# The order of fills, row maxima and weight splits in a hybrid DeltaNet and attention block

## The reference

```python
h = rmsnorm(x, norm_w[l])
proj = jnp.einsum('bsd,de->bse', h, w_in[l])
y_a = gated_deltanet(gdn_qkv, gdn_z, gdn_b, gdn_a, ...)
y_b = forgetting_attention(fox_q, fox_k, fox_v, fox_z, fox_f, ...)
g_a, g_b = jnp.split(jax.nn.sigmoid(gate_logit + gate_b[l]), 2, axis=-1)
merged = g_a * (y_a @ w_up_gdn[l]) + g_b * (y_b @ w_up_fox[l])
x = x + merged @ w_out[l]
return rmsnorm(x, final_norm_w)
```

## Time and profile before

| | |
|---|---|
| median of 3 runs | 1018.75 us (1017.97 to 1020.62) |
| the profiled execution, its own time | 1018.75 us |
| its span, first to last instruction | 1016.8 us |
| mean granted TensorE clock | 0.993 |
| TensorE busy | 960.7 us, 94% |
| VectorE, ScalarE busy | 604.8 us (59%), 464.6 us (46%) |
| edited loop, by TensorE | some 532 to 790 us |

### The profile page before, as it was taken

One profiled execution on the slowest core, in us unless ns is written; L12 is line 12 of the kernel. 1 busy time (PEld: TensorE's weight loads), 2 busy tenths in 40 slices (PEclk: granted clock), 3 DMA queues, 4 the chain that ended last, 5 costly groups with the idle time before them and its releaser, 6 DMA issues.

```text
span 1016.8 us, 15520 instructions
## 1 busy us (share of the span) xinstructions
PE 960.7 (94%) x6224; PEld 730.3 (72%) x6224; DVE 604.8 (59%) x949; ACT 464.6 (46%) x847; POOL 20.7 (2%) x28
## 2 busy tenths in 40 slices
PE   3899999999999999999789989999899999999997
PEld 2777787778888877777566656665565788888886
DVE  6367658799999623343368476675774342328162
ACT  6355655533555435422346546546455543334041
POOL 1000001020000000000000000000000000000000
PEclk9999999999999999999899999999999999999999
DMA  6111351148223662210453332333210523233062
GB/s 212 42 46 51 88 178 44 59 149 210 84 83 104 207 198 60 68 54 33 146 167 101 98 114 74 115 104 104 81 65 22 208 77 100 68 119 104 2 205 83
DMA packets 115039, 104.85 MB, mean 103 GB/s; under 512 B 33488, under 2 KB 95056, under 8 KB 114584
## 3 DMA queue, kind: packets, MB, share of 16 engines
q1 hardware_dynamic: 103304, 80.26, 27.0%
q10 hardware_dynamic: 10512, 19.40, 5.2%
q0 software_dynamic: 1152, 4.19, 1.3%
HBM read 76.84 MB, written 27.00 MB: 102 GB/s over the span
## 4 chain that ended last, share of the span: by engine, by line
PE 43%; ACT 3%; DVE 2%; issue 2%; DMA 1%; DVEq 0%; SPq 0%; ACTq 0%
PE pj L2042 6%; PE pj L2044 5%; PE pj L2043 5%; PE pc L2170 3%; PE pa L2143 2%; PE pa L2112 1%; PE pj L2053 1%; PE pj L2054 1%; PE pj L2055 1%; PE pb L2185 1%; DMA mst<-rows_scratch 1%; PE pb L2196 1%; PE pc L2307 1%; PE pb L2307 1%; PE pa L2307 1%
## 5 line engine op out<-in xcount | busy, mean ns | idle before, releaser
L143 PE MATMUL pj<-h_hi,w_hi 128*128 128x512 f32 x496 | 199.4, 402 | 4.2 <-ACT xc L492 2.3
L145 PE MATMUL pj<-h_hi,w_lo 128*128 128x512 f32 x496 | 193.6, 390 | 0.0
L144 PE MATMUL pj<-h_lo,w_hi 128*128 128x512 f32 x496 | 193.4, 390 | 0.0
L143 PEld LDWEIGHTS pj<-h_hi,w_hi 128*128 128x128 f32 x496 | 93.0, 188 | 27.8 <-issue 5.3
L2042 PE MATMUL pj<-h_hi,w_hi 128*128 128x512 f32 x256 | 107.2, 419 | 3.4 <-PEq L292 3.4
L145 PEld LDWEIGHTS pj<-h_hi,w_lo 128*128 128x128 f32 x496 | 93.1, 188 | 19.9
L144 PEld LDWEIGHTS pj<-h_lo,w_hi 128*128 128x128 f32 x496 | 93.2, 188 | 17.6
L2044 PE MATMUL pj<-h_hi,w_lo 128*128 128x512 f32 x256 | 101.7, 397 | 0.0
L2043 PE MATMUL pj<-h_lo,w_hi 128*128 128x512 f32 x256 | 101.5, 396 | 0.0
L2042 PEld LDWEIGHTS pj<-h_hi,w_hi 128*128 128x128 f32 x256 | 49.2, 192 | 25.9 <-issue 16.2
L599 ACT ACTIVATE xc<-pj 128x512 f32<-128x512 f32 x40 | 23.8, 596 | 94.5 <-PE pj L145 94.5
(11 more groups left out here) (317 smaller groups left out, 1836.3 us busy)
## 6 DMA issues: line engine op xcount, KB each, us to landing
w_raw<-in_w_in SPq DMA_DIRECT2D x48, 512.0 KB, 4.5
fox_scratch<-xc ACTq DMA_DIRECT2D x40, 256.0 KB, 2.1
qkv<-in_x SPq DMA_DIRECT2D x8, 512.0 KB, 6.8
fqk<-fox_scratch SPq DMA_DIRECT2D x8, 512.0 KB, 4.4
fa<-rows_scratch POOLq DMA_DIRECT2D x8, 512.0 KB, 5.5
rv<-fr_scratch SPq DMA_DIRECT2D x16, 256.0 KB, 4.1
m_scratch<-mst ACTq DMA_DIRECT2D x16, 256.0 KB, 2.8
ma<-m_scratch SPq DMA_DIRECT2D x8, 512.0 KB, 4.3
```

The costliest lines, as they stand in the source:

```text
L143: nc.tensor.matmul(o, w_hi[:, slot, k], h_hi[:, k, cols], start=(k == 0), stop=False)
L144: nc.tensor.matmul(o, w_hi[:, slot, k], h_lo[:, k, cols], start=False, stop=False)
L145: last = nc.tensor.matmul(o, w_lo[:, slot, k], h_hi[:, k, cols], start=False, stop=(k == KT - 1))
```

## The change

The count of operations on each engine stays as it was, and so does `FILLS`. TensorE: the eight fills around `turn_max(p, 0)` are 3, 4, 1 instead of 4, 4; in steps v = 0 to 3 the fills stand between slot v's scores and the short piece, and the values (or `turn_values`) behind the short piece; at v = 3 two fills stand there and two behind; `values(p, 3)` comes behind the next two slots' scores; `weight_sums(p, 0)` and `head_sums(p + 1)` change places, with the waits for the shared bank that go with it. ScalarE: the work on z is a step later, `squares`, `row_norms` two steps later, `sum_square(2 p)` two earlier. VectorE: the work on z stands behind the row maxima, `out_y(p - 1, 1)` ahead of `spread_max(p, 1)`, the output norm of the first half at v = 6 instead of 8, `normalise` at v = 10 and 11 instead of 8 and 10, `add_weights(p, 5)` a step earlier; the low parts of weights are made one step earlier. SP: loads of weights one step earlier and ahead of the norms in the queue, `load_v` ahead of `norm_rows`, both at v = 8 instead of 5, `norm_rows_k` at v = 10 instead of 8.

```diff
@@ SP
+                    for t in tiles_through(g - 2):
+                        load_raw(t + 3)
+                    for t in ups_through(g - 2):
+                        load_up(t + 3)
                     if v == 4 and p:
                         store_y(p - 1, 1)
-                    if v == 5 and p + 1 < PAIRS:
+                    if v == 8 and p + 1 < PAIRS:
+                        load_v(p + 1)
                         norm_rows(p + 1)
-                        load_v(p + 1)
-                    if v == 8 and p + 1 < PAIRS:
+                    if v == 10 and p + 1 < PAIRS:
                         norm_rows_k(p + 1)
-                    for t in tiles_through(g - 3):
-                        load_raw(t + 3)
-                    for t in ups_through(g - 3):
-                        load_up(t + 3)
@@ ScalarE
-                        if v == 1:
+                        if v == 2:
                             act.wait_ge(fz_loaded, 16 * p + 16)
...
-                        if v == 2:
+                        if v == 3:
                             act.wait_ge(z_step, 2 * p + 1)
...
-                        if v == 3 and p + 1 < PAIRS:
+                        if v == 5 and p + 1 < PAIRS:
                             squares(p + 1, 0, fq, q_loaded)
                             squares(p + 1, 1, fk, k_loaded)
-                        if v == 5 and p + 1 < PAIRS:
+                        if v == 5:
+                            sum_square(2 * p)
+                        if v == 7 and p + 1 < PAIRS:
                             row_norms(p + 1)
-                        if v == 7:
-                            sum_square(2 * p)
@@ VectorE
-                        if v >= 1 and slot(v - 1)[1] and v != 6:
-                            if v == 7:
-                                add_weights(p, 5)
+                        if v >= 1 and slot(v - 1)[1]:
                             add_weights(p, v - 1)
                         if 0 <= v < 4:
                             row_max(p, 4 + 2 * v)
-                            if v == 2:
-                                dve.wait_ge(z_act, 3 * p + 1)
-                                nc.vector.tensor_scalar(fv, fv, LN_MAX, 1.0, ALU.min, ALU.add).then_inc(z_step, 1)
-                            if v == 3:
-                                dve.wait_ge(z_act, 3 * p + 3)
-                                nc.vector.scalar_tensor_tensor(fz, fz, fox_nw["o"], fv, ALU.mult, ALU.mult).then_inc(z_step, 1)
                             row_max(p, 5 + 2 * v)
...
                     if g < STEPS:
+                        if v == 2:
+                            dve.wait_ge(z_act, 3 * p + 1)
+                            nc.vector.tensor_scalar(fv, fv, LN_MAX, 1.0, ALU.min, ALU.add).then_inc(z_step, 1)
                         if v == 3:
-                            spread_max(p, 1)
                             if p:
                                 out_y(p - 1, 1)
-                        if v == 8:
-                            if p + 1 < PAIRS:
-                                normalise(p + 1, 0)
+                            spread_max(p, 1)
+                        if v == 4:
+                            dve.wait_ge(z_act, 3 * p + 3)
+                            nc.vector.scalar_tensor_tensor(fz, fz, fox_nw["o"], fv, ALU.mult, ALU.mult).then_inc(z_step, 1)
+                        if v == 6:
                             add_squares(2 * p)
                             out_gate(p, 0)
                         if v == 10 and p + 1 < PAIRS:
-                            normalise(p + 1, 1)
+                            normalise(p + 1, 0)
                         if v == 11:
                             out_y(p, 0)
+                        if v == 11 and p + 1 < PAIRS:
+                            normalise(p + 1, 1)
...
-                    for t in tiles_through(g - 2):
+                    for t in tiles_through(g - 1):
                         split_w_lo(t + 2)
-                    for t in ups_through(g - 2):
+                    for t in ups_through(g - 1):
                         split_up_lo(t + 2)
@@ TensorE
-                        pe.wait_ge(r_made, 2 * p)
+                        pe.wait_ge(den_sq, 2 * p - 1)
...
-                    elif p + 1 < PAIRS:
-                        pe.wait_ge(frow_act, 2 * (p + 1) + 1)
...
                     if h == 0:
-                        pe.wait_ge(den_sq, 2 * p + 1)
+                        if p + 1 < PAIRS:
+                            pe.wait_ge(frow_act, 2 * (p + 1) + 1)
...
-                    fill(4)
+                    fill(3)
                     max_scores(p, 2)
                     max_scores(p, 3)
                     turn_values(p, 0)
                     fill(4)
                     turn_max(p, 0)
+                    fill(1)
                     for v in range(4):
                         max_scores(p, 4 + 2 * v)
                         key_scores(p, v)
                         past_only(p, v)
+                        fill(4 if v < 3 else 2)
+                        max_scores(p, 5 + 2 * v)
                         if v == 0:
                             turn_values(p, 1)
                         else:
                             values(p, v - 1)
-                        max_scores(p, 5 + 2 * v)
                         if v == 1 and p:
                             square_sums(p - 1, 1)
-                        fill(4)
+                    fill(2)
                     turn_max(p, 1)
                     for v in range(4, SLOTS, 2):
-                        if v == 4:
-                            values(p, 3)
                         key_scores(p, v)
                         key_scores(p, v + 1)
...
                         if v == 4:
-                            if p + 1 < PAIRS:
+                            values(p, 3)
+                            weight_sums(p, 0)
+                        else:
+                            if v == 6 and p + 1 < PAIRS:
                                 head_sums(p + 1)
-                        else:
-                            if v == 6:
-                                weight_sums(p, 0)
                             values(p, v - 2)
                             values(p, v - 1)
```

## The result

The changed kernel takes 1051.29 us in the median (1049.76 to 1056.26), the kernel before 1019.01 us: a ratio of 1.0324, 95% interval 1.0287 to 1.0361, 33 us slower. The forecast was 1040 us with a range of 1025 to 1050: right in direction, too small, and the time lies outside the range.

What follows compares the result with a forecast made beforehand. TensorE, busy 94% of the span, was taken as the bound. Added 30.4 us less removed 10.4 gave net 20.0, plus 1.6 for the clock, on 1018.75: 1040 us, own range 1032 to 1045, 8-in-10 range 1025 to 1050.

Steps and rivals of the forecast that it cites:

- The short piece loses its cover: TensorE before key_scores and turn_max(p, 1): fewer products stand between short piece and bank reuse; 8.5 us added over four pairs.
- The covers gained: Moved fills cover TensorE's waits: 2.1 us before key_scores in pairs 1 to 3, 5.2 us before max_scores removed.
- The split: VectorE's earlier split_w_lo waits for ScalarE's split_w_hi, delaying row maxima and add_weights; 11.1 us of TensorE waits added.
- The last long piece: VectorE does L1917, adds and scans before reading long piece 10, so TensorE waits; 4.0 us added.
- The chain of norms: Later head_sums and row_norms delay the next pair's first max_scores: 2.3, 0.85 and 2.0 us in pairs 0 to 2.
- the upper end: Norm store queued behind load_v and a weight tile in pair 2: up to 2.4 us more; 0 was taken.
- The sum of the waits: All TensorE waits in the loop, without edges and clock: 20.6 us more.
- The failed step: the clock: TensorE's granted clock: one fall to half speed removed (1.6 us), one added by new waits (1.6 us).
- the clock falls at many waits: Rival: five more falls of TensorE's clock at waits, 1.6 us each; 1048 us, chance 0.17.
- The covers win: Rival: short piece's row maximum is ready when key_scores comes, only the 10.4 us gain counts; 1008 us, chance 0.06.
- savings cancel: Rival: waits on w_hi vanish and only half the others come, cancelling the savings; 1019 us, chance 0.04.
- the split does not bite: Rival: ScalarE has w_hi ready during the four fills, so 11.1 and 2.3 us fall away; 1025 us, chance 0.13.

Runs made afterwards that it cites:

- e6: Changed kernel with the low parts of the weights back at their old step on VectorE, weight loads still early: 1035.8 us, ratio 1.0163.
- e7: Changed kernel with load_v put behind norm_rows in SP's list: 1049.51 us, ratio 1.0309.
- e3: Kernel before with only the norm operations (and load_v) moved as in the change, on all engines: 1026.51 us, ratio 1.0073.
- e5: Changed kernel with 14 and 20 idle products ahead of the first max_scores of pairs 1 and 3: 1045.43 us, ratio 1.0262.
- e1: Kernel before with only TensorE's new order of v = 0 to 3 and the 3, 4, 1 fills: 1024.68 us, ratio 1.0071.
- e2: Kernel before with only the low parts of weights (VectorE) and weight loads (SP) one step earlier: 1041.05 us, ratio 1.0219.
- e4: Kernel before with the norm operations moved and the work on z a step later on ScalarE and VectorE: 1032.46 us, ratio 1.0128.
- e9: Kernel before with idle products, 5 at pair 1's first max_scores, 6 before key_scores(0) of pairs 1 to 3: 1014.48 us, ratio 0.997.

## Why the prediction was right in direction and too small

*The short piece loses its cover.* Right: 6.1 us in the change, 6.8 us alone, against 7.3 before `key_scores`; the 256-column piece waited only in pair 0, 0.5 us, as said. *The covers gained.* Right: 0.7 us for each wait for L1785, the first wait before a short piece gone.

*The split.* Right, place by place: 1.4, 2.2, 3.0, 2.2, 1.8 us measured against 1.3, 2.3, 2.9, 2.3, 2.3, and 2.4 us against 2.3 at the next pair. e6 took these 13 us of waits away, and 3.6 us came in their place.

*The last long piece.* Wrong in its parts, and right only in sum: 4.0 us forecast, and 3.95 us measured in pair 2 alone, 0.35 us or less in pairs 0, 1 and 3. The step took L1917 as a price of 0.69 us and did not ask what it waits for; it waits for ScalarE's exponential of the same step. In pairs 0 and 3 the wait on the split came just ahead, and what was to stand between was done meanwhile: the forecast charged both, and e6 shows that it had the place right, for without the split these waits are 1.8 us each, 1.5 forecast.

*The chain of norms.* Right in pairs 0 and 1 (2.4 and 0.8 us against 2.3 and 0.85). In pair 2 the wait was 5.4 us; the 2.4 us for the store behind 1 MB of loads, kept as the upper end, had to be in the sum. e7 and e3 showed that it is the loads ahead in the queue: with the weight tile alone ahead the wait was 3.1 us, with neither 2.5 us.

*The sum of the waits* is right in part by luck. Too little was charged for the norms in pair 2 (3.4 us) and for z in pair 2 (3.3 us); too much for the last long piece elsewhere (3.3 us), for `turn_max` (2.0 us) and for the short pieces (1.2 us).

*The failed step: the clock.* Waits came to 20.5 us against 20.6. For the clock the sum had -1.6 for the fall removed and +1.6 for one more, together nothing, though the kernel before had two falls in the loop and not one. The profile has 32 us more at half speed, 30.6 of them in the loop. The loop is 35.8 us longer; without 20.5 us of waits and 1.0 for edges 14 us are left, and this is what the term for the clock should have been, or somewhat less. It can be reckoned without this difference: some 3.4 of the 30.6 us lie in the waits near 594 and 749 us, and the others, at the 0.47 us that the starts of products show, make 12.8 us. By e5's price of 0.33 us it is 10 us. The other runs bear it out, each against the kernel before, between the same two products:

| run | loop longer, us | waits (and idle products) more | at 1.2 GHz more |
|---|---|---|---|
| e1, order | 5.8 | 4.8 | -3.4 |
| e2, split | 25.1 | 13.1 | 27.2 |
| e3, norms | 10.7 | 2.8 | 17.0 |
| e4, norms and z | 12.9 | 7.7 | 10.2 |
| e9, before with idle products | -2.7 | 0.0 | -6.8 |
| e6, change without the split | 19.8 | 13.8 | 6.8 |
| e5, change with idle products | 29.3 | 21.2 | 10.2 |
| the change | 35.8 | 20.5 | 30.6 |

In e2, e3, e4 and e9, which have TensorE's old order, what waits don't explain is 0.40 to 0.51 us for each us at 1.2 GHz. The runs with the new order have some 2.6 us on top, which e1 shows alone and no wait accounts for: the forecast's 1.0 for edges is the place for it. The medians close too: 33 us, less 20.5 of waits and 1.0 to 2.6 for edges, leaves 10 to 11.5 us for some 25 us at half speed in the mean. The single executions of the changed kernel, all of one program, have 0.981 and a span of 1047.7 us at one end, 0.972 and 1054.2 us at the other, 0.34 us for each us at half speed.

So the rival *the clock falls at many waits* was the case. Its price of 1.6 us for each fall was right for a fall as in the earlier trace rows; it counted five more falls, and that is what the profile has, seven against two, but four of the seven are of double length. The Trainium skill (TensorE: Matmul & The Clock Gate, A second HAM failure mode: psum-queue depth-cycling) has the rule on short idle times between groups that the forecast weighed. This case agrees with it only in that the clock did fall more often: e1 has nine waits of up to 1.0 us before `key_scores` and no fall at them. Of the seven falls of the change six stand at waits of 1.8 us and more, and one, at 610 us, behind waits of 0.89 and 0.76 us; the same two waits in e5 had none.

*Rivals that fell.* The covers win, savings cancel, the split does not bite: none came. That SP's earlier loads gain nothing was not tried alone; they are in e2 and e6 alike.

What stays open: which waits make the clock fall, and for how long. The same 1.6 us wait of the kernel before was followed by a fall in one pair of three, and the clock of one kernel differs between executions (0.990 to 0.998 in e9). The 2.6 us of TensorE's new order have no row either.

## What to carry to other kernels

When an operation is moved, ask for each engine that runs in order what the operation waits for in its new place, not only what it costs there: two operations of 1.2 and 0.7 us kept VectorE waiting for 2.3 to 3.5 us because their producer stood late in the same step. Price waits of TensorE of 2 us and more with the clock that they take along, here 10 to 14 us on top of 20. And compare clocks over many executions: one profile of each kernel put the growth at half speed at 32 us where the mean was 25. Where a wait can't be removed, products that nobody reads kept the clock up, where a bank was free to take them: 0.3% in a kernel that was 94% busy. And a small transfer that others wait for goes ahead of large loads in its queue.

## What the hardware showed that I had not expected

Adding work made kernels faster: 34 products of 128 x 512 took 6 us off the changed kernel, 23 products took 3 to 4 us off the kernel before. Stretches at half speed in the loop lasted 3.4 or 6.8 us, and the length of the wait did not decide which: the wait of 3.77 us had 6.8 us, the wait of 3.95 us 3.4 us, and in e3 two waits of 1.57 us had 6.8 us each.
